# High and low activation parts side by side, and the last up projection with one wide high-weight matmul per block

## The chip, the cores and the metric

The kernel runs on one core of one Trainium2 chip. The number of interest is the device time of one launch in microseconds (us). TensorE (PE in the profile, its weight loads PEld) multiplies, VectorE (DVE), ScalarE (ACT) and GpSimd (POOL) do the elementwise work, SyncE (SP) issues the weight transfers.

## The reference

Three layers run on one sequence of 256 tokens and 1024 features, in float32: two layers of a first block (retention and differential attention, each with a memory attention beside it) and one layer of a second block (a state-space mixer beside forgetting attention). Each layer ends with a gated MLP. The change is in the last one:

```python
def conv_gated_mlp(x, w_up, conv_w, conv_b, w_down):
    h = x @ w_up.astype(x.dtype)
    h = causal_depthwise_conv(h, conv_w, conv_b)
    gate, val = jnp.split(h, 2, axis=-1)
    return (jax.nn.silu(gate) * val) @ w_down.astype(x.dtype)
```

Its input is `rms_norm_2(x, norm_ffn_w)`, `w_up` is 1024 x 5632, the convolution has 3 taps along the tokens and a bias, `w_down` is 2816 x 1024.

## The kernel before

Activations lie feature-major: 128 features on the partitions, T = 256 tokens along the row. Every weight is split into a rounded high part and the rest (low), every activation too, and a product is high x high + high x low + low x high, all in the format fp32r (the trace prints it as f32 or fp32r). For each block of 128 input features TensorE therefore has two forms in `products`:

- **separate** (L728, L729, L730): high weight on the high activation, high weight on the low activation, low weight on the high activation: three matmuls of 256 columns with three weight loads, all summed in one half of a PSUM bank;
- **joined** (L726, L730): the high weight goes over both activation parts at once, 512 columns, and leaves two sums in the two halves of the bank; then the low weight on the high activation, 256 columns. Two weight loads. Somebody has to add the two halves afterwards.

The joined form is used for the names in `HALVES`: the up projections of the first two layers and most of the down projections. All high parts of a buffer lie in its first half and all low parts in its second; `hi_and_lo` makes the view of 512 columns out of two runs of 256.

A projection goes through its weight tiles one by one (`project` on TensorE). `up2`, the last up projection, has 44 weight tiles of 8 blocks, gate and value tiles in turn, four tiles per turn of a loop, the first turn written out. While tile c is evacuated, the engines do this for it:

- SyncE loads the raw weight tile into a ring of 4. ScalarE rounds it to the high part (`split_hi`, L1163), VectorE subtracts (`split_lo`, L1653), both three tiles ahead of TensorE.
- VectorE evacuates the sum of tile c times the reciprocal root mean square (`rstd`) into one of two rows of `halo` (`halo_evac`, L1794).
- ScalarE does the last tap and the bias (`last_tap`, L1266), VectorE the other two taps of tile c-1 (`other_taps`, L1803, twice; the second waits for the first), and then `split_lo`.
- On value tiles ScalarE also takes the silu of the gate tile before (L1239) and rounds the product of the pair before (`ffn_split`, L1234); GpSimd multiplies silu and value (L1596) and subtracts the rounded product (`lo`, L1573), once per pair of tiles. `down2` reads what comes out.

Each engine works strictly in the order written; what it waits for are counters (semaphores). In the first two layers' up projections (`up0`, `up1`) ScalarE copies the second half of the PSUM bank to `low_half` (`copy_low`, L1246), VectorE adds (L1771, L1775), and GpSimd multiplies by the root (L1581).

Of the kernel before, what the change touches and what calls it, by code (L numbers as in the profile page):

```python
# [23 lines left out]
P = 128  # L24
T = 256
# [90 lines left out]
HALVES = ("up0", "up1", "down0", "down1", "down2")  # L116
# [218 lines left out]
def program(nc, x_in, mem_in, params_in, consts_in, w, out):  # L335
# [9 lines left out]
    with ExitStack() as ctx:  # L345
# [11 lines left out]
        act_hi, act_lo = act_parts[:, 0:FT * T], act_parts[:, FT * T:2 * FT * T]  # L357
        xw_hi, xw_lo = xw_parts[:, 0:KT * T], xw_parts[:, KT * T:2 * KT * T]
# [11 lines left out]
        small_r = act_hi[:, 20 * T:22 * T]  # L370
# [73 lines left out]
        x_first, low_copied, gate_summed, silu_scaled = sem("x_first"), sem("low_copied"), sem("gate_summed"), sem("silu_scaled")  # L444
# [57 lines left out]
        def tok(buf, c0, width, tt):  # L502
# [4 lines left out]
        NORMS = [("mem", "kv", act_hi, act_lo), ("attn0", "in0", xw_hi, xw_lo), ("ffn0", "up0", xw_hi, xw_lo),  # L507
                 ("attn1", "in1", xw_hi, xw_lo), ("ffn1", "up1", xw_hi, xw_lo), ("mix2", "in2", xw_hi, xw_lo),
                 ("ffn2", "up2", xw_hi, xw_lo)]
# [207 lines left out]
        def _(pe):  # L717
            mm = nc.tensor.matmul

            def products(ps, a, parts, t, start, stop, halves=False):  # L720


                w_hi, w_lo = ring_hi[:, a:a + P], ring_lo[:, a:a + P]
                x_parts = hi_and_lo(parts, t * T)
                if halves:
                    mm(ps[:, 0:2 * T], w_hi, x_parts, start=start, stop=False)  # L726
                else:
                    mm(ps[:, 0:T], w_hi, x_parts[:, 0, :], start=start, stop=False)  # L728
                    mm(ps[:, 0:T], w_hi, x_parts[:, 1, :], start=False, stop=False)  # L729
                return mm(ps[:, 0:T], w_lo, x_parts[:, 0, :], start=False, stop=stop)  # L730

            def project(ph, i, c, parts, ready, halfway=None):
# [12 lines left out]
                if ph.by_token(c):  # L745
                    second = c not in ph.wide
                    for k in range(4):
                        if halfway and k == 2:
                            halfway(c)
                        t = ph.inputs[4 * second + k]  # L750
                        a = slot * DM + k * T
                        w_hi, w_lo = ring_hi[:, a:a + T], ring_lo[:, a:a + T]
                        for tt in range(2):
                            o = bank[b][:, tt * T:(tt + 1) * T]
                            x_tok = hi_and_lo(parts, t * T + tt * P, P)
                            mm(o, x_tok[:, 0, :], w_hi, start=not second and k == 0 and tt == 0, stop=False)  # L756
                            mm(o, x_tok[:, 0, :], w_lo, start=False, stop=False)  # L757
                            last = mm(o, x_tok[:, 1, :], w_hi, start=False, stop=second and k == 3 and tt == 1)  # L758
                    last.then_inc(tile_done, 1)
                    return  # L760
# [381 lines left out]
        def _(act):  # L1142
# [23 lines left out]
            def stream_hi(q, m, src):  # L1166
                name, _, hi, _ = NORMS[q]
                A(tile(hi, m), tile(src, m), ACT.Copy, scale=pcol(name, m)).then_inc(xh_done, 1)
# [24 lines left out]
            def run(name, after=None, q=None, unrolled=False, end=None):  # L1193

                ph = PH[name]
                peeled = ph.turns if unrolled else 1
                for i in range(peeled):
                    for c in range(ph.body):
                        for j, d in split_steps(ph, i, c):
                            split_hi(ph, j, d)  # L1200
                        if c == 0 and i == 0 and q is not None:
                            inverse_root(q)
                        if after:
                            after(ph, i, c)
                if peeled < ph.turns:
                    with act.Fori(peeled, ph.turns) as i:
                        for c in range(ph.body):
                            split_hi(ph, i, c)
# [23 lines left out]
            def ffn_split(p, h, f):  # L1232
                act.wait_ge(prod_done, p + 1)
                A(tile(act_hi, f), two(prod, h), ACT.Copy).then_inc(ffn_hi, 1)  # L1234
# [6 lines left out]
            def copy_low(layer, ph, i, c):  # L1241

                act.wait_ge(tile_done, ph.tile(i, c)[1] + 1)
                if not (type(i) is int and c < 2):
                    act.wait_ge(out_ready, ph.out(i, c) - 1)
                A(two(low_half, c % 2), bank[ph.bank(i, c)][:, T:2 * T], ACT.Copy).then_inc(low_copied, 1)  # L1246

            def swiglu(layer):
                def after(ph, i, c):
                    h = c // 2  # L1250
                    p = FT * layer + 2 * i + h
                    copy_low(layer, ph, i, c)
# [7 lines left out]
            def last_tap(n, taps, j, n_conv, b):  # L1260

                act.wait_ge(out_ready, n + 1)
# [114 lines left out]
            def values(layer, kind, h):  # L1377
# [8 lines left out]
                A(tile(act_hi, t - 12), bank[6][:, 0:T], ACT.Copy).then_inc(vals_hi, 1)  # L1386

            def mix(layer, k):

                t = mixed_tile(act, layer, k)  # L1390
                A(tile(act_hi, k), tile(u, t), ACT.Copy).then_inc(mix_hi, 1)

            def mix_high(layer, k):

                t = mixed_tile(act, layer, k)
                A(tile(act_hi, k, 2 * T), tile(u, t, 2 * T), ACT.Copy).then_inc(pair_hi, 1)
# [56 lines left out]
            def fox_values(layer, p):  # L1453
                act.wait_ge(fx_o, p + 1)
                A(tile(act_hi, 8 + p), bank[6][:, 0:T], ACT.Copy).then_inc(fx_hi, 1)
# [92 lines left out]
            run("up2", conv_swiglu, 6, end=lambda: ffn_split(3 * FT - 1, 1, FT - 1))  # L1548
# [4 lines left out]
        def _(pool):  # L1553
# [17 lines left out]
            def lo(p, h, f):  # L1571
                pool.wait_ge(ffn_hi, p + 1)
                G.tensor_tensor(tile(act_lo, f), two(prod, h), tile(act_hi, f).bitcast(f32), SUB).then_inc(ffn_lo, 1)  # L1573
# [15 lines left out]
            def conv_ffn():  # L1589
                def product(i, h):  # L1590
# [6 lines left out]
                    lo(p, h, 2 * i + h)  # L1597
                for h in range(2):
                    product(0, h)
                with pool.Fori(1, FT // 2) as i:  # L1600
                    for h in range(2):
                        product(i, h)

            def mix(layer, k):
                pool.wait_ge(mix_hi, number["mix", (layer, k)] + 1)
                G.tensor_tensor(tile(act_lo, k), tile(u, mixed_tile(None, layer, k)),
                                tile(act_hi, k).bitcast(f32), SUB).then_inc(mix_lo, 1)
# [30 lines left out]
        def _(dve):  # L1638
# [151 lines left out]

            def halo_evac(ph, i, c, ps):
# [121 lines left out]
            def mix_low(layer, k):  # L1913
# [3 lines left out]
                V.tensor_tensor(tile(act_lo, k, 2 * T), tile(u, t, 2 * T), tile(act_hi, k, 2 * T).bitcast(f32),  # L1917
# [133 lines left out]
            def fox_values(layer, p):  # L2051
                dve.wait_ge(fx_hi, p + 1)
                V.tensor_tensor(tile(act_lo, 8 + p), bank[6][:, 0:T], tile(act_hi, 8 + p).bitcast(f32),
# [95 lines left out]
            run("up2", halo_evac, None, 6, before_split=conv_before, end=conv_end)  # L2149
# [105 lines left out]
```

## Time and profile before

| | |
|---|---|
| median of 3 runs | 1058.32 us (1050.75 to 1058.38) |
| profiled execution | 1054.23 us |
| its span in the trace | 1052.4 us |
| TensorE busy | 1033.7 us (98%) |
| VectorE busy | 792.3 us (75%) |
| ScalarE busy | 636.9 us (61%) |
| GpSimd busy | 233.8 us (22%) |
| `up2` on TensorE | 858.40 to 985.54 us |

The granted TensorE clock is 1.00 of full speed in every stretch asked for, and in the page's row of slices. Matmul durations in the trace contain the time in the pipe, so what one costs in a stream is read from start to start. A span on VectorE, ScalarE or GpSimd is likewise longer than the distance to the next start by 0.04 to 0.10 us.

### The profile page before, as it was taken

How to read it: one execution, taken by the hardware profiler on the slowest of the kernel's cores; microseconds unless marked ns; L12 is line 12 of the kernel's file. 1: busy time of each engine (PE TensorE's matmuls, PEld its weight loads, DVE VectorE, ACT ScalarE, POOL GpSimd, SP SyncE). 2: the span in 40 equal slices, each digit the busy share in tenths (PEclk: the TensorE clock that was granted, in tenths of full speed). 3: DMA queues.
4: the chain of work that ended last, by engine and by line, in shares of the span. 5: the costliest groups of instructions: out<-in, count | busy, mean ns of one | idle time of the engine just before them, and what ended most of it. 6: DMA issues, size and time to landing. Idle time of an engine off the chain costs nothing.

```text
span 1052.4 us, 22106 instructions
## 1 busy us (share of the span) xinstructions
PE 1033.7 (98%) x7484; PEld 945.9 (90%) x7484; DVE 792.3 (75%) x1315; ACT 636.9 (61%) x1188; POOL 233.8 (22%) x204
## 2 busy tenths in 40 slices
PE   7999999999999999999999998999999999999998
PEld 7999988888889888888888898999898999999888
DVE  6875897777665878987786668878867579888853
ACT  7654775665545676766665446665666666666532
POOL 3200044454110000244452110000101034444300
PEclk9999999999999999999999999999999999999999
DMA  8543476556665332666566654443343456555563
GB/s 296 181 138 94 132 221 196 182 180 187 188 187 180 126 106 72 200 200 193 185 184 196 187 174 158 148 156 121 114 128 120 128 166 190 179 179 179 169 211 101
DMA packets 52484, 174.37 MB, mean 166 GB/s; under 512 B 5952, under 2 KB 7232, under 8 KB 52288
## 3 DMA queue, kind: packets, MB, share of 16 engines
q1 hardware_dynamic: 52416, 173.46, 52.6%
q8 instruction: 44, 0.72, 0.3%
q14 instruction: 24, 0.20, 0.1%
HBM read 172.39 MB, written 1.05 MB: 165 GB/s over the span
## 4 chain that ended last, share of the span: by engine, by line
PE 73%; DVE 13%; issue 6%; ACT 4%; DVEq 1%; DMA 1%; POOL 0%; ACTq 0%; SPq 0%; POOLq 0%
PE scores L726 14%; PE bank L730 13%; PE bank L726 12%; PE bank L728 8%; PE scores L730 7%; PE bank L729 7%; DVE tmp L1803 5%; DVE ring_parts L1653 3%; PE bank L756 2%; PE bank L757 1%; PE bank L758 1%; DVE con L1794 1%; ACT ring_parts L1163 1%; PE scores L971 1%; DMA ring_raw<-w_up 1%
## 5 line engine op out<-in xcount | busy, mean ns | idle before, releaser
L1653 DVE TENSOR_TENSOR ring_parts<-ring_raw,ring_parts 128x1024 fp32r<-128x1024 f32 (+2 forms) x343 | 421.8, 1232 | 38.3 <-ACT ring_parts L1163 32.1
L1163 ACT ACTIVATE ring_parts<-ring_raw 128x1024 fp32r<-128x1024 f32 (+2 forms) x343 | 341.0, 998 | 62.7 <-PE scores L730 29.3
L730 PE MATMUL bank<-xw_parts,ring_parts 128*128 128x256 f32 x1048 | 295.3, 282 | 0.0
L728 PE MATMUL bank<-xw_parts,ring_parts 128*128 128x256 f32 x696 | 202.6, 291 | 1.1 <-DVE ring_parts L1653 0.6
L730 PEld LDWEIGHTS bank<-xw_parts,ring_parts 128*128 128x128 f32 x1048 | 199.6, 190 | 0.0
L729 PE MATMUL bank<-xw_parts,ring_parts 128*128 128x256 f32 x696 | 196.7, 283 | 0.0
L730 PE MATMUL scores<-xw_parts,ring_parts 128*128 128x256 f32 x528 | 148.5, 281 | 0.0
L728 PEld LDWEIGHTS bank<-xw_parts,ring_parts 128*128 128x128 f32 x696 | 133.0, 191 | 6.8 <-issue 5.1
L730 PE MATMUL bank<-act_parts,ring_parts 128*128 128x256 f32 x480 | 135.2, 282 | 0.0
L729 PEld LDWEIGHTS bank<-xw_parts,ring_parts 128*128 128x128 f32 x696 | 133.1, 191 | 0.1
L726 PE MATMUL scores<-xw_parts,ring_parts 128*128 128x512 f32 x352 | 125.0, 397 | 0.6 <-DVE xw_parts L1659 0.6
L726 PE MATMUL bank<-xw_parts,ring_parts 128*128 128x512 f32 x352 | 124.5, 395 | 0.4 <-DVE xw_parts L1659 0.4
L730 PEld LDWEIGHTS scores<-xw_parts,ring_parts 128*128 128x128 f32 x528 | 100.3, 190 | 0.1
L1573 POOL TENSOR_TENSOR act_parts<-tmp,act_parts 128x256 f32 (+1 forms) x66 | 61.6, 934 | 168.6 <-ACT act_parts L1234 168.6
L730 PE MATMUL scores<-act_parts,ring_parts 128*128 128x256 f32 x336 | 94.4, 281 | 0.0
L726 PE MATMUL scores<-act_parts,ring_parts 128*128 128x512 f32 x264 | 93.1, 396 | 0.7 <-DVE ring_parts L1653 0.7
L730 PEld LDWEIGHTS bank<-act_parts,ring_parts 128*128 128x128 f32 x480 | 91.4, 190 | 0.0
L728 PE MATMUL bank<-act_parts,ring_parts 128*128 128x256 f32 x282 | 81.5, 289 | 2.7 <-DVE ring_parts L2098 1.4
L726 PEld LDWEIGHTS scores<-xw_parts,ring_parts 128*128 128x128 f32 x352 | 66.0, 187 | 16.5 <-DVE xw_parts L1659 1.2
L726 PEld LDWEIGHTS bank<-xw_parts,ring_parts 128*128 128x128 f32 x352 | 66.0, 187 | 16.2 <-DVE xw_parts L1659 0.9
L729 PE MATMUL bank<-act_parts,ring_parts 128*128 128x256 f32 x282 | 79.7, 283 | 0.0
L1581 POOL TENSOR_TENSOR tmp<-tmp,rstd 128x256 f32<-128x256 f32 x44 | 74.2, 1688 | 9.3 <-ACT tmp L1239 9.2
(245 smaller groups left out, 1928.8 us busy)
## 6 DMA issues: line engine op xcount, KB each, us to landing
ring_raw<-w_up SPq DMA_DIRECT2D x132, 512.0 KB, 3.6
ring_raw<-w_in SPq DMA_DIRECT2D x85, 512.0 KB, 3.5
ring_raw<-w_down SPq DMA_DIRECT2D x48, 512.0 KB, 3.6
ring_raw<-w_down SPq DMA_DIRECT2D x24, 384.0 KB, 4.0
ring_raw<-w_oa SPq DMA_DIRECT2D x16, 256.0 KB, 2.6
ring_raw<-w_ob SPq DMA_DIRECT2D x16, 256.0 KB, 2.9
ring_raw<-w_oa SPq DMA_DIRECT2D x8, 512.0 KB, 3.5
ring_raw<-w_ob SPq DMA_DIRECT2D x8, 512.0 KB, 3.5
```

The costliest lines, as they stand in the source:

```text
L726: mm(ps[:, 0:2 * T], w_hi, x_parts, start=start, stop=False)
L728: mm(ps[:, 0:T], w_hi, x_parts[:, 0, :], start=start, stop=False)
L729: mm(ps[:, 0:T], w_hi, x_parts[:, 1, :], start=False, stop=False)
L730: return mm(ps[:, 0:T], w_lo, x_parts[:, 0, :], start=False, stop=stop)
L756: mm(o, x_tok[:, 0, :], w_hi, start=not second and k == 0 and tt == 0, stop=False)
L757: mm(o, x_tok[:, 0, :], w_lo, start=False, stop=False)
L758: last = mm(o, x_tok[:, 1, :], w_hi, start=False, stop=second and k == 3 and tt == 1)
L1163: A(ring_hi[:, slot * DM:slot * DM + width], ring_raw[:, slot * DM:slot * DM + width], ACT.Copy).then_inc(hi_done, 1)
L1573: G.tensor_tensor(tile(act_lo, f), two(prod, h), tile(act_hi, f).bitcast(f32), SUB).then_inc(ffn_lo, 1)
L1581: G.tensor_tensor(two(gate_s, h), two(gate_s, h), rstd[:, :], MUL).then_inc(silu_scaled, 1)
L1653: V.tensor_tensor(ring_lo[:, a:b], ring_raw[:, a:b], ring_hi[:, a:b].bitcast(f32), SUB).then_inc(lo_done, 1)
L1803: V.scalar_tensor_tensor(dst, halo[:, b * 264 + 3 - s:b * 264 + 259 - s], pcol(wname, j * taps + taps - 2 - s), acc, MUL, ADD).then_inc(do ...
```

## The change

1. The parts buffers are laid out anew: the high part of a tile (256 columns) is followed by its low part. The 512 columns of a joined matmul are now one run. `high`, `low`, `pair_of` and `pair_tiles` take the place of `hi_and_lo` and the two half buffers, in all stages. Which instructions run is not touched by this.
2. `up2` joins `HALVES`. TensorE uses the joined form. ScalarE copies the second half of the bank at the start of each tile's work (`first=copy_low`). VectorE adds the halves into `halo` (`halo_sum`) where it multiplied by the root. GpSimd multiplies the row by the root in place (`scaled`), and ScalarE's last tap waits for that.
3. GpSimd's order in `up2`: the product and the subtraction of a pair come one pair later, between the `scaled` of the next two tiles.

```diff
-HALVES = ("up0", "up1", "down0", "down1", "down2")
+HALVES = ("up0", "up1", "up2", "down0", "down1", "down2")
...
-        def hi_and_lo(parts, a, width=T):
-
-            return parts[:, :].rearrange("p (n c) -> p n c", n=2)[:, :, a:a + width]
+        def high(parts, k):
+
+            return parts[:, ds(k * (2 * T), T)]
+
+        def low(parts, k):
+            return parts[:, ds(k * (2 * T) + T, T)]
...
-                x_parts = hi_and_lo(parts, t * T)
                 if halves:
-                    mm(ps[:, 0:2 * T], w_hi, x_parts, start=start, stop=False)
+                    mm(ps[:, 0:2 * T], w_hi, tile(parts, 2 * t, 2 * T), start=start, stop=False)
...
                     with act.Fori(peeled, ph.turns) as i:
                         for c in range(ph.body):
+                            if first:
+                                first(ph, i, c)
                             split_hi(ph, i, c)
...
-                act.wait_ge(out_ready, n + 1)
+                if taps == 4:
+                    act.wait_ge(out_ready, n + 1)
+                else:
+                    act.wait_ge(halo_scaled, j + 1)
...
-            run("up2", conv_swiglu, 6, end=lambda: ffn_split(3 * FT - 1, 1, FT - 1))
+            run("up2", conv_swiglu, 6, end=lambda: ffn_split(3 * FT - 1, 1, FT - 1), first=copy_low)
...
             def conv_ffn():
+                def scaled(i, c):
+                    n = 4 * i + c
+                    pool.wait_ge(out_ready, PH["up2"].out0 + n + 1)
+                    row = halo[:, (c % 2) * 264 + 4:(c % 2) * 264 + 260]
+                    G.tensor_tensor(row, row, rstd[:, :], MUL).then_inc(halo_scaled, 1)
+
...
-                    lo(p, h, 2 * i + h)
+
+                def pair(i, h):
+
+                    before = not (type(i) is int and i == 0 and h == 0)
+                    scaled(i, 2 * h)
+                    if before:
+                        product(i if h else i - 1, 1 - h)
+                    scaled(i, 2 * h + 1)
+                    if before:
+                        lo(2 * FT + 2 * i + h - 1, 1 - h, 2 * i + h - 1)
...
+            def halo_sum(ph, i, c, ps):
+                b = c % 2
+                dve.wait_ge(low_copied, 4 * FT + 4 * i + c + 1)
+                V.tensor_tensor(halo[:, b * 264 + 4:b * 264 + 260], ps, two(low_half, b), ADD).then_inc(out_ready, 1)
...
-            run("up2", halo_evac, None, 6, before_split=conv_before, end=conv_end)
+            run("up2", halo_sum, None, 6, before_split=conv_before, end=conv_end)
```

ScalarE's order in the first turn of `up2`, tiles 1 to 3, before (L1163 `split_hi`, L1239 silu, L1234 `ffn_split`, L1266 last tap):

```order
L1163 ACTIVATE ring_parts<-ring_raw 128x1024 [waits tile_done,w_loaded2]
L1266 ACTIVATE tmp<-con,par 128x256 [waits conv_b,out_ready]
L1163 ACTIVATE ring_parts<-ring_raw 128x1024 [waits tile_done,w_loaded3]
L1239 ACTIVATE tmp<-tmp 128x256 [waits prod_done,conv_d]
L1234 ACTIVATE act_parts<-tmp 128x256 [waits prod_done]
L1266 ACTIVATE tmp<-con,par 128x256 [waits conv_b,out_ready]
```

And now (L1171 `split_hi`, L1253 silu, L1248 `ffn_split`, L1283 last tap, L1260 `copy_low`):

```order
L1260 ACTIVATE u<-scores 128x256 [waits out_ready,tile_done]
L1171 ACTIVATE ring_parts<-ring_raw 128x1024 [waits tile_done,w_loaded2]
L1283 ACTIVATE tmp<-con,par 128x256 [waits conv_b,halo_scaled]
L1260 ACTIVATE u<-bank 128x256 [waits out_ready,tile_done]
L1171 ACTIVATE ring_parts<-ring_raw 128x1024 [waits tile_done,w_loaded3]
L1253 ACTIVATE tmp<-tmp 128x256 [waits prod_done,conv_d]
L1248 ACTIVATE act_parts<-tmp 128x256 [waits prod_done]
L1283 ACTIVATE tmp<-con,par 128x256 [waits conv_b,halo_scaled]
```

A copy stands ahead of each `split_hi`, behind the last tap of the tile before, and the last tap waits for GpSimd instead of VectorE.

GpSimd's order in the first turn of `up2`, before (L1569 is the last work ahead of it, L1596 the product, L1573 `lo`):

```order
L1569 TENSOR_TENSOR scratch<-scratch 128x256 [waits ss_done,sq_done] x7
L1596 TENSOR_TENSOR tmp<-tmp 128x256 [waits conv_d,silu_done]
L1573 TENSOR_TENSOR act_parts<-tmp,act_parts 128x256 [waits ffn_hi]
L1596 TENSOR_TENSOR tmp<-tmp 128x256 [waits conv_d,silu_done]
L1573 TENSOR_TENSOR act_parts<-tmp,act_parts 128x256 [waits ffn_hi]
```

And now (L1611 `scaled`, L1619 the product, L1590 `lo`):

```order
L1586 TENSOR_TENSOR scratch<-scratch 128x256 [waits ss_done,sq_done] x7
L1611 TENSOR_TENSOR con<-con,rstd 128x256 [waits out_ready] x3
L1619 TENSOR_TENSOR tmp<-tmp 128x256 [waits conv_d,silu_done]
L1611 TENSOR_TENSOR con<-con,rstd 128x256 [waits out_ready]
L1590 TENSOR_TENSOR act_parts<-tmp,act_parts 128x256 [waits ffn_hi]
```

Two instructions per pair of tiles have become four, each with two inputs in SBUF.

## Rows read from the trace of the kernel before

**Rows 1.** The page: busy time and share, and the chain by engine

```profile
PE 1033.7 (98%) x7484; PEld 945.9 (90%) x7484; DVE 792.3 (75%) x1315; ACT 636.9 (61%) x1188; POOL 233.8 (22%) x204
PE 73%; DVE 13%; issue 6%; ACT 4%; DVEq 1%; DMA 1%; POOL 0%; ACTq 0%; SPq 0%; POOLq 0%
```

**Rows 2.** Windows in `up0` and `up2`: PE, PEld, DVE, ACT, POOL, clock, DMA

```profile
150.00:220.00 70.00, 70.00 (x398) 60.68 (x397) 55.73 (x76) 43.82 (x76) 34.05 (x26) 1.00 0.59 188
870.00:985.00 115.00, 115.00 (x961) 115.00 (x960) 102.96 (x159) 71.80 (x121) 53.94 (x40) 1.00 0.58 181
```

**Rows 3.** Timeline of PE: start, duration; `up2` separate, to `down2`'s first

```profile
913.54 0.28 PE L728 MATMUL bank<-xw_parts,ring_parts 128*128 128x256 f32 x1
...
919.30 0.28 PE L728 MATMUL scores<-xw_parts,ring_parts 128*128 128x256 f32 x1
...
985.54 0.40 PE L726 MATMUL bank<-act_parts,ring_parts 128*128 128x512 f32 x1
```

**Rows 4.** Timeline of PE in `up0`, joined

```profile
175.99 0.40 PE L726 MATMUL scores<-xw_parts,ring_parts 128*128 128x512 f32 x1
176.22 0.28 PE L730 MATMUL scores<-xw_parts,ring_parts 128*128 128x256 f32 x1
...
181.64 0.40 PE L726 MATMUL bank<-xw_parts,ring_parts 128*128 128x512 f32 x1
```

**Rows 5.** Timeline of PE: one run of 384 columns, then two of 128

```profile
686.04 0.33 PE L1081 MATMUL bank<-act_parts,pick_r 128*128 128x384 f32 x1
686.21 0.28 PE L1082 MATMUL bank<-ident_r,mask_r 128*128 128x256 f32 x1
686.33 0.28 PE L728 MATMUL bank<-xw_parts,ring_parts 128*128 128x256 f32 x1
```

**Rows 6.** Timeline of DVE in `up2`: start, duration; one tile, then the next

```profile
908.59 0.42 DVE L1794 TENSOR_TENSOR con<-bank,rstd 128x256 f32<-128x256 f32 x1
908.92 0.63 DVE L1803 SCALAR_TENSOR_TENSOR tmp<-con,par,tmp 128x256 f32<-128x256 f32 x1
909.70 0.48 DVE L1803 SCALAR_TENSOR_TENSOR tmp<-con,par,tmp 128x256 f32<-128x256 f32 x1 [0.15 <-DVE tmp L1803]
910.31 1.23 DVE L1653 TENSOR_TENSOR ring_parts<-ring_raw,ring_parts 128x1024 fp32r<-128x1024 f32 x1
911.45 0.42 DVE L1794 TENSOR_TENSOR con<-scores,rstd 128x256 f32<-128x256 f32 x1
```

**Rows 7.** Timeline of POOL: `up2` beside VectorE, and the stage's last

```profile
908.29 0.97 POOL L1573 TENSOR_TENSOR act_parts<-tmp,act_parts 128x256 f32 x1 [1.89 <-ACT act_parts L1234]
910.34 1.78 POOL L1596 TENSOR_TENSOR tmp<-tmp 128x256 f32<-128x256 f32 x1 [1.08 <-DVE tmp L1803]
...
992.81 0.73 POOL L1573 TENSOR_TENSOR act_parts<-tmp,act_parts 128x256 f32 x1 [0.72 <-ACT act_parts L1234]
```

**Rows 8.** Timeline of ACT: `copy_low` in `up0`; silu to `split_hi` in `up2`

```profile
176.27 0.39 ACT L1246 ACTIVATE u<-bank 128x256 f32<-128x256 f32 x1 [1.36 <-PE bank L730]
...
913.28 0.42 ACT L1239 ACTIVATE tmp<-tmp 128x256 f32<-128x256 f32 x1 [2.32 <-DVE tmp L1803]
913.91 0.59 ACT L1266 ACTIVATE tmp<-con,par 128x256 f32<-128x256 f32 x1
914.40 1.04 ACT L1163 ACTIVATE ring_parts<-ring_raw 128x1024 fp32r<-128x1024 f32 x1
```

**Rows 9.** Timeline of DVE in `up0`: a sum, and `split_lo` beside POOL

```profile
176.69 0.42 DVE L1771 TENSOR_TENSOR tmp<-bank,u 128x256 f32<-128x256 f32 x1 [0.94 <-ACT u L1246]
...
177.49 1.76 DVE L1653 TENSOR_TENSOR ring_parts<-ring_raw,ring_parts 128x1024 fp32r<-128x1024 f32 x1
```

**Rows 10.** Timeline of POOL in `up0`: the instruction beside it

```profile
177.25 0.92 POOL L1573 TENSOR_TENSOR act_parts<-tmp,act_parts 128x256 f32 x1 [3.12 <-ACT act_parts L1234]
```

**Rows 11.** Timeline of DVE: `up2`'s first and last evacuation

```profile
864.39 0.42 DVE L1794 TENSOR_TENSOR con<-bank,rstd 128x256 f32<-128x256 f32 x1
...
986.84 0.42 DVE L1794 TENSOR_TENSOR con<-bank,rstd 128x256 f32<-128x256 f32 x1
```

More of the change, by code:

```diff
@@ L503, in tok @@
             return buf[:, tt * DM + c0:tt * DM + c0 + width]
-        NORMS = [("mem", "kv", act_hi, act_lo), ("attn0", "in0", xw_hi, xw_lo), ("ffn0", "up0", xw_hi, xw_lo),
-                 ("attn1", "in1", xw_hi, xw_lo), ("ffn1", "up1", xw_hi, xw_lo), ("mix2", "in2", xw_hi, xw_lo),
-                 ("ffn2", "up2", xw_hi, xw_lo)]
+        NORMS = [("mem", "kv", act_parts), ("attn0", "in0", xw_parts), ("ffn0", "up0", xw_parts),
+                 ("attn1", "in1", xw_parts), ("ffn1", "up1", xw_parts), ("mix2", "in2", xw_parts),
+                 ("ffn2", "up2", xw_parts)]
         LAST_Q = {0: 1, 1: 3, 2: 5}
@@ L754, in project @@
                             o = bank[b][:, tt * T:(tt + 1) * T]
[L755 to L758, printed above, removed]
+                            x_hi, x_lo = (m(parts, t)[:, tt * P:(tt + 1) * P] for m in (high, low))
+                            mm(o, x_hi, w_hi, start=not second and k == 0 and tt == 0, stop=False)
+                            mm(o, x_hi, w_lo, start=False, stop=False)
+                            last = mm(o, x_lo, w_hi, start=False, stop=second and k == 3 and tt == 1)
                     last.then_inc(tile_done, 1)
@@ L1191, in inverse_root, with run @@
                 A(rstd[:, :], logs, ACT.Exp, scale=-0.5).then_inc(root_done, 1)
-            def run(name, after=None, q=None, unrolled=False, end=None):
+            def run(name, after=None, q=None, unrolled=False, end=None, first=None):
                 ph = PH[name]
@@ L1198, in run @@
                     for c in range(ph.body):
+                        if first and (i or c):
+                            first(ph, i, c)
                         for j, d in split_steps(ph, i, c):
@@ L1202, in run @@
                             inverse_root(q)
+                            if first:
+                                first(ph, i, c)
                         if after:
@@ L1207, in run @@
                         for c in range(ph.body):
+                            if first:
+                                first(ph, i, c)
                             split_hi(ph, i, c)
@@ L1233, in ffn_split @@
                 act.wait_ge(prod_done, p + 1)
-                A(tile(act_hi, f), two(prod, h), ACT.Copy).then_inc(ffn_hi, 1)
+                A(high(act_parts, f), two(prod, h), ACT.Copy).then_inc(ffn_hi, 1)
             def silu_gate(p, h, src):
@@ L1251, in after @@
                     p = FT * layer + 2 * i + h
-                    copy_low(layer, ph, i, c)
+                    copy_low(ph, i, c)
                     if c % 2 == 0:
@@ L1454, in fox_values @@
                 act.wait_ge(fx_o, p + 1)
-                A(tile(act_hi, 8 + p), bank[6][:, 0:T], ACT.Copy).then_inc(fx_hi, 1)
+                A(high(act_parts, 8 + p), bank[6][:, 0:T], ACT.Copy).then_inc(fx_hi, 1)
             def fox_weights(layer, p):
@@ L1572, in lo @@
                 pool.wait_ge(ffn_hi, p + 1)
-                G.tensor_tensor(tile(act_lo, f), two(prod, h), tile(act_hi, f).bitcast(f32), SUB).then_inc(ffn_lo, 1)
+                G.tensor_tensor(low(act_parts, f), two(prod, h), high(act_parts, f).bitcast(f32), SUB).then_inc(ffn_lo, 1)
             def ffn(layer):
```

49 lines of the change are left out of this document (27 added, 22 removed).

## The prediction, made before the changed kernel ran

> **What bounds the kernel now.** I read the page first. TensorE is busy 98% of the span and carries 73% of the chain of waits; VectorE carries 13% [rows 1]. That says "TensorE" for the whole, but the change puts its new work into `up2`, so the windows come next: in a stretch of `up2` TensorE is busy all 115 us, and VectorE 103 of 115, against 56 of 70 in `up0` [rows 2]. Then the timelines, engine by engine.
>
> TensorE in `up2` goes from one tile pair to the next in 919.30 - 913.54 = 5.76 us, 48 matmuls of 0.120 us each [rows 3]. In `up0` the joined form takes 181.64 - 175.99 = 5.65 us for 32 matmuls [rows 4], so a joined tile costs 2.82 us and a separate one 2.88. That is all that joining can give as measured: 0.055 x 44 = 2.4 us.
>
> VectorE does one tile of `up2` in 911.45 - 908.59 = 2.86 us, four instructions with one gap of 0.15 us [rows 6]. It is as slow as TensorE. Whatever lengthens its step sets the pace of the stage.
>
> Why a step is 2.86: the first of the two taps takes 0.63 us, the second 0.48 [rows 6]. While the first runs, GpSimd is finishing an instruction that began at 908.29 and ends at 909.26; the tap ends 0.29 us after that, at 909.55 [rows 6, 7]. The reverse is seen too: GpSimd's product starts at 910.34, 0.03 us after `split_lo`, and takes 1.78 us where an undisturbed GpSimd instruction takes 0.73; it ends 0.58 us after `split_lo` does (912.12 against 911.54) [rows 6, 7]. In `up0` a `split_lo` that starts 0.24 us after a GpSimd instruction takes 1.76 us in place of 1.23, and ends 1.08 us after it [rows 6, 9, 10]. So an instruction of GpSimd and one of VectorE with two inputs in SBUF go one after the other. VectorE's evacuation has one input in PSUM, takes 0.42 us beside GpSimd's product, and is free of this [rows 6, 7].
>
> **The change, part by part.**
>
> *TensorE in `up2`*: 44 tiles at 2.82 in place of 2.88, at best -2.4 us. It is worth nothing if VectorE's step is longer than 2.82, and it is already.
>
> *VectorE*: the multiplication by the root becomes a sum of the same shape with one input in PSUM, 0.42 us as in `up0` [rows 9]. No count changes.
>
> *GpSimd*: 44 instructions more, `scaled`, each 0.73 us alone. Two per pair of tiles have become four, and all of them take turns with the taps and `split_lo`.
>
> *ScalarE*: 44 copies of 0.39 us [rows 8]. ScalarE has time for 44 x 0.39 = 17 us (72 of 115 busy, [rows 2]), but the copy of tile c stands behind the last tap of tile c-1, and VectorE's sum of tile c waits for it.
>
> I lay out a pair of steps, t = 0 at the start of VectorE's sum.
>
> *Gate tile*: tap 1 starts at 0.33 and ends at 0.82 (0.48 when undisturbed). `scaled` waits from 0.58 (the sum's end plus 0.16, as the product starts 0.16 after the tap's end at 910.18). Between the two taps there is the gap of 0.15 us, so GpSimd goes in and ends at 0.82 + 0.58 = 1.40. Tap 2 ends 0.29 later, 1.69. `split_lo` starts 0.13 later (910.31 - 910.18), 1.82, and the next sum 1.14 after that (911.45 - 910.31): **2.96 us**.
>
> *Value tile*: `split_lo` of the step before ends at 0.09 by this tile's clock, so the product ends at 0.67 and tap 1 at 0.96; `scaled`, behind the product, ends at 1.54; tap 2 at 1.83. ScalarE starts the silu 0.12 later at 1.95, the last tap 0.63 after that (913.91 - 913.28) at 2.58, the next tile's copy 0.49 later (914.40 - 913.91) at 3.07; it ends at 3.46, and VectorE sums 0.03 later (176.69 against 176.66) [rows 8, 9]: **3.49 us**. VectorE alone would be free at 3.10; the other 0.39 is the chain through ScalarE.
>
> A pair is 6.45 us. From the first to the last evacuation of `up2` it is now 986.84 - 864.39 = 122.4 us [rows 11]; 43 steps become 21.5 x 6.45 = 138.7, **+16.3 us**. Does the end pass it on? `down2` starts on TensorE at 985.54 [rows 3], comes to its last two blocks after some 20 x 0.353 = 7.1 us and needs them by 993; the last of them is ready at 992.81 + 0.73 = 993.54 [rows 7]. There is no slack, so it passes on in full. The bounds: if GpSimd's instructions cost VectorE nothing beyond today's, the gate step is 2.86 and the value step 0.33 + 0.63 + 0.15 + 0.48 = 1.59, plus the same 1.66 through ScalarE, 3.25: a pair of 6.11, +9.0 us. If the product gets in ahead of `split_lo` (they start 0.03 us apart) it costs VectorE 0.53 more per pair, as in `up0`: +27 us. The register instructions that the new waits bring are in no row; the gap of 0.15 us in a loop shows their size, once or so per pair, up to +3 us. I take +16.3, since each of its terms is the duration of the same instruction beside the same neighbour.
>
> *The layout*: 1166 joined matmuls outside `up2` (2 x 352 in `up0` and `up1`, 3 x 154 in the down projections, by the code) read one run of 512 columns in place of two of 256. No row shows such a read. A joined pair takes 0.353 us, of which L730 is 0.120 or a little less, so the wide one is 0.23 [rows 4]. From below: two runs of 128 (L1082) take 0.12 [rows 5], the same as one run of 256, so a second run costs nothing there. From above: one run of 384 takes 0.17 [rows 5]; 128 columns more at the full clock of 2.4 GHz (granted 1.00, [rows 2]) are 0.053, together 0.224, 0.01 under what is measured. So 0 to 10 ns each, 0 to 11.7 us. I take 3 ns, nearer to the row that has two runs in it: **-3.5 us**. Those stages would turn it into time, since TensorE bounds them: VectorE has 14 of 70 us free in `up0`.
>
> The Trainium skill (TensorE: Matmul & The Clock Gate, "Wait — 56ns, not 53.3ns?") gives a warm 512-column matmul 215.7 ns from start to start, without a word on how the columns lie. By it a joined pair is worth some 18 ns more than its row shows, and if the two runs are the reason the sum would be 21 us lower. The 0.120 us of every 256-column matmul, with one run, stand against 109 by the same formula, so the trace does not bear that out.
>
> *Sum*: 1054.2 (profiled execution) + 16.3 - 3.5 = **1067 us**. That execution is 4.1 us under the median of the runs; against the median the same sum gives 1071.
>
> **The rivals.**
>
> 1. *One run is read at the row of 384's rate* (10 ns each): 1054.2 + 16.3 - 11.7 = 1059. For it: the wide matmul carries twice the overhead of the one of 384. Against: two runs of 128 cost nothing extra. 25%.
> 2. *GpSimd's new instructions fit beside VectorE*, and only ScalarE's chain is left: 1054.2 + 9.0 - 3.5 = 1060. For it: `scaled` is issued while VectorE sums from PSUM. Against: it can start only when that sum has ended, and then tap 1 is ahead of it. 14%.
> 3. *Faster*: the four GpSimd instructions fall into VectorE's free moments, the value step shrinks to the undisturbed chain 0.33 + 2 x 0.5 + 1.66 = 2.99, TensorE's 5.65 per pair paces the stage (121.5 us, -0.9), and the layout gives its whole 11.7: 1042. It decides if VectorE's pair comes under 5.65; four turns of 0.58 us in the 0.66 us of two sums speak against it. 10%.
> 4. By the page's figure with the slow `up2`: 0.018 x 1166 = 21 us off, 1054.2 + 16.3 - 21 = 1049.5. 4%.
> 5. *The product overtakes `split_lo`*: 1054.2 + 27 - 3.5 = 1078. 5%.
>
> My forecast keeps 42%, its own range is 1063 to 1074 (layout 0 to 6 ns, registers up to 3 us).
>
> **The numbers.** 1050 to 1077 leaves out rivals 3 to 5 (19%) and takes in the two bounds of the layout and of the stage. What a measurement of this kernel can tell from no change is about 1%, 10.6 us. The forecast is +12.8, over that in most of its range (36 of 42), and rival 5 too; rival 1 at +4.8 and rival 2 at +5.8 lie within, with 7 of 39 over it if the layout gives less and the registers cost. Slower by over 1%: 0.48; within 1%: 0.40; faster by over 1%: 0.12 (rival 3 and part of 4).
>
> **What would show it.** In `up2` of the changed kernel: VectorE's distance from sum to sum 2.96 and 3.49 in turn; `scaled` 0.8 to 0.95 us long and ending between the taps; TensorE waiting in its tiles, VectorE waiting on ScalarE's copy on every second tile; the stage 16 us longer. In `up0`: a pair of tiles in 5.60 us for 3 ns, 5.49 for 10 ns, 5.65 if the layout does nothing. I am wrong if the pair of `up2` comes under 6.1 us, or if `up0` gains over 0.1 us per pair.

## The result, and the profile after

| | before | after |
|---|---|---|
| median, runs side by side on one chip | 1054.53 us (4 runs, 1050.29 to 1058.38) | 1067.49 us (4 runs, 1066.66 to 1070.41) |
| ratio to before | | 1.0138 (95% interval 1.0106 to 1.0169) |
| profiled execution, span | 1054.23, 1052.4 us | 1067.06, 1065.3 us |
| VectorE's first to last evacuation of `up2` | 122.45 us | 137.98 us |

The changed kernel is 13 us (1.4%) slower; 1067.0 was forecast. The interval of the ratio lies wholly above 1%.

The page of the changed kernel: busy time, then the chain by engine.

```profile
PE 1040.2 (98%) x7132; PEld 925.3 (87%) x7132; DVE 801.9 (75%) x1315; ACT 651.9 (61%) x1232; POOL 273.2 (26%) x248
PE 74%; DVE 12%; ACT 5%; issue 4%; DMA 1%; DVEq 1%; ACTq 1%; POOL 0%; SPq 0%; POOLq 0%
```

Beside [rows 1] this tells almost nothing. TensorE has 352 matmuls fewer (44 tiles of 8 blocks) and is still busy 98%, and GpSimd is on 0% of the chain. The windows, of `up0` and `up2` as in [rows 2], tell more:

```profile
150.00:220.00 70.00, 70.00 (x406) 61.22 (x406) 56.96 (x77) 44.12 (x76) 34.17 (x26) 1.00 0.62 192
870.00:998.00 128.00, 122.20 (x639) 97.07 (x638) 111.68 (x160) 85.23 (x160) 89.16 (x80) 1.00 0.51 161
```

In `up2` TensorE had no idle time and now idles 5.8 of 128 us; GpSimd has gone from 54 busy of 115 to 89 of 128. VectorE does 160 instructions in 128 us, before 159 in 115. The granted clock is 1.00 in both.

One pair of tiles on VectorE (start, duration, in brackets the idle time before and who ended it), as [rows 6]. L1828 is the sum, L1842 the two taps, L1687 `split_lo`:

```profile
922.55 0.42 DVE L1828 TENSOR_TENSOR con<-bank,u 128x256 f32<-128x256 f32 x1
922.89 0.62 DVE L1842 SCALAR_TENSOR_TENSOR tmp<-con,par,tmp 128x256 f32<-128x256 f32 x1
923.67 0.72 DVE L1842 SCALAR_TENSOR_TENSOR tmp<-con,par,tmp 128x256 f32<-128x256 f32 x1 [0.15 <-DVE tmp L1842]
924.51 1.23 DVE L1687 TENSOR_TENSOR ring_parts<-ring_raw,ring_parts 128x1024 fp32r<-128x1024 f32 x1
925.94 0.42 DVE L1828 TENSOR_TENSOR con<-bank,u 128x256 f32<-128x256 f32 x1 [0.21 <-ACT u L1260]
926.28 0.48 DVE L1842 SCALAR_TENSOR_TENSOR tmp<-con,par,tmp 128x256 f32<-128x256 f32 x1
926.91 0.73 DVE L1842 SCALAR_TENSOR_TENSOR tmp<-con,par,tmp 128x256 f32<-128x256 f32 x1 [0.15 <-DVE tmp L1842]
927.77 1.22 DVE L1687 TENSOR_TENSOR ring_parts<-ring_raw,ring_parts 128x1024 fp32r<-128x1024 f32 x1
928.91 0.42 DVE L1828 TENSOR_TENSOR con<-scores,u 128x256 f32<-128x256 f32 x1
```

GpSimd beside it, as [rows 7]: L1611 `scaled`, L1590 `lo`, L1619 the product.

```profile
923.19 0.92 POOL L1611 TENSOR_TENSOR con<-con,rstd 128x256 f32<-128x256 f32 x1
925.36 0.97 POOL L1590 TENSOR_TENSOR act_parts<-tmp,act_parts 128x256 f32 x1 [1.25 <-ACT act_parts L1248]
926.45 0.91 POOL L1611 TENSOR_TENSOR con<-con,rstd 128x256 f32<-128x256 f32 x1
927.81 1.78 POOL L1619 TENSOR_TENSOR tmp<-tmp 128x256 f32<-128x256 f32 x1 [0.45 <-DVE tmp L1842]
```

And ScalarE in the value step, as [rows 8]: silu, `ffn_split`, last tap, the next tile's copy.

```profile
924.42 0.42 ACT L1253 ACTIVATE tmp<-tmp 128x256 f32<-128x256 f32 x1 [1.36 <-DVE tmp L1842]
924.75 0.40 ACT L1248 ACTIVATE act_parts<-tmp 128x256 f32 x1
925.05 0.59 ACT L1283 ACTIVATE tmp<-con,par 128x256 f32<-128x256 f32 x1
925.55 0.36 ACT L1260 ACTIVATE u<-bank 128x256 f32<-128x256 f32 x1
```

The reader is to see three things. The second tap takes 0.72 us in every step, where it took 0.48: `scaled` starts 0.30 us after the first tap does and ends at 924.11, and the second tap ends 0.28 us later. The steps are 925.94 - 922.55 = 3.39 us (value; 3.51 on every second one) and 928.91 - 925.94 = 2.97 us (gate). And in the value step VectorE is free 0.21 us before ScalarE's copy is: that copy stands behind silu, `ffn_split` and last tap, and the first of them, the silu, waits for the second tap.

The waits of the same stretch, 870 to 998 us (total, times, longest):

```profile
ACT tmp L1283 <- POOL con L1611: 15.4, 20, 0.8
...
DVE con L1828 <- ACT u L1260: 5.6, 20, 0.5
PE scores L734 <- DVE ring_parts L1687: 3.2, 10, 0.5
...
PE bank L734 <- DVE ring_parts L1687: 1.9, 10, 0.3
```

The largest entry, ScalarE's 15.4 us for `scaled`, looks like the culprit and is not: it falls in gate steps, where ScalarE has time. The 5.6 us on VectorE are 20 times 0.28, once per value step.

The end of the stage: VectorE's last evacuation (the first is at 861.55), GpSimd's last subtraction, TensorE's first block of `down2`, and its wait for the last activation block.

```profile
999.53 0.42 DVE L1828 TENSOR_TENSOR con<-bank,u 128x256 f32<-128x256 f32 x1
```

```profile
1005.49 0.73 POOL L1590 TENSOR_TENSOR act_parts<-tmp,act_parts 128x256 fp32r<-128x256 f32 x1 [0.53 <-ACT act_parts L1248]
```

```profile
996.28 0.49 PE L734 MATMUL bank<-act_parts,ring_parts 128*128 128x512 f32 x1
...
1006.27 0.51 PE L734 MATMUL bank<-act_parts,ring_parts 128*128 128x512 f32 x1 [1.48 <-POOL act_parts L1590]
```

The last subtraction on GpSimd ends 6.69 us after the last evacuation began, before 6.70 [rows 7, 11]. So whatever VectorE loses in `up2` arrives at the end.

Where the 12.9 us of span came from: the first evacuation of `up2` is 2.84 us earlier (861.55 against 864.39), the 43 steps to the last take 15.53 us longer, and the rest 0.2.

### The profile page after: what moved, and what is told of

Its sections match the earlier page's. It is cut to its first block, busy times and chain, and to the rows that moved or that the text cites. A ratio compares the mean times of both kernels' runs of the same rounds, so it can differ in the third digit from the quotient of the medians.

```text
span 1065.3 us, 21665 instructions
## 1 busy us (share of the span) xinstructions
PE 1040.2 (98%) x7132; PEld 925.3 (87%) x7132; DVE 801.9 (75%) x1315; ACT 651.9 (61%) x1232; POOL 273.2 (26%) x248
## 4 chain that ended last, share of the span: by engine, by line
PE 74%; DVE 12%; ACT 5%; issue 4%; DMA 1%; DVEq 1%; ACTq 1%; POOL 0%; SPq 0%; POOLq 0%
PE scores L734 14%; PE bank L738 13%; PE bank L734 12%; PE bank L736 8%; PE scores L738 7%; PE bank L737 7%; DVE tmp L1842 5%; DVE ring_parts L1687 3%; PE bank L764 2%; PE bank L765 1%; PE bank L766 1%; ACT ring_parts L1171 1%; DMA ring_raw<-w_up 1%; PE scores L979 1%; DVE con L1828 1%
## 5 line engine op out<-in xcount | busy, mean ns | idle before, releaser
L1687 DVE TENSOR_TENSOR ring_parts<-ring_raw,ring_parts 128x1024 fp32r<-128x1024 f32 (+2 forms) x343 | 422.0, 1233 | 38.6 <-ACT ring_parts L1171 32.9
L1171 ACT ACTIVATE ring_parts<-ring_raw 128x1024 fp32r<-128x1024 f32 (+2 forms) x343 | 341.2, 998 | 62.8 <-PE scores L738 28.6
L738 PE MATMUL bank<-xw_parts,ring_parts 128*128 128x256 f32 x1048 | 293.6, 280 | 0.0
L738 PEld LDWEIGHTS bank<-xw_parts,ring_parts 128*128 128x128 f32 x1048 | 198.6, 189 | 0.0
L734 PE MATMUL scores<-xw_parts,ring_parts 128*128 128x512 f32 x528 | 188.8, 400 | 4.2 <-DVE ring_parts L1687 3.2
L734 PE MATMUL bank<-xw_parts,ring_parts 128*128 128x512 f32 x528 | 188.1, 399 | 3.5 <-DVE ring_parts L1687 2.4
L736 PE MATMUL bank<-xw_parts,ring_parts 128*128 128x256 f32 x520 | 152.8, 294 | 1.1 <-DVE ring_parts L1687 0.6
L737 PE MATMUL bank<-xw_parts,ring_parts 128*128 128x256 f32 x520 | 146.9, 282 | 0.0
L734 PEld LDWEIGHTS scores<-xw_parts,ring_parts 128*128 128x128 f32 x528 | 99.0, 188 | 33.3 <-issue 9.7
L734 PEld LDWEIGHTS bank<-xw_parts,ring_parts 128*128 128x128 f32 x528 | 99.0, 188 | 32.7 <-issue 9.1
L736 PEld LDWEIGHTS bank<-xw_parts,ring_parts 128*128 128x128 f32 x520 | 99.2, 191 | 6.8 <-issue 5.1
L1590 POOL TENSOR_TENSOR act_parts<-tmp,act_parts 128x256 f32 (+1 forms) x66 | 61.1, 926 | 151.9 <-ACT act_parts L1248 151.9
L737 PEld LDWEIGHTS bank<-xw_parts,ring_parts 128*128 128x128 f32 x520 | 99.3, 191 | 0.1
L738 PEld LDWEIGHTS scores<-xw_parts,ring_parts 128*128 128x128 f32 x528 | 99.3, 188 | 0.1
L1842 DVE SCALAR_TENSOR_TENSOR tmp<-con,par,tmp 128x256 f32<-128x256 f32 x124 | 73.8, 595 | 7.1 <-DVE tmp L1842 6.1
```

The lines of the kernel that those rows point to most:

```text
L734: mm(ps[:, 0:2 * T], w_hi, tile(parts, 2 * t, 2 * T), start=start, stop=False)
L736: mm(ps[:, 0:T], w_hi, high(parts, t), start=start, stop=False)
L737: mm(ps[:, 0:T], w_hi, low(parts, t), start=False, stop=False)
L738: return mm(ps[:, 0:T], w_lo, high(parts, t), start=False, stop=stop)
L1171: A(ring_hi[:, slot * DM:slot * DM + width], ring_raw[:, slot * DM:slot * DM + width], ACT.Copy).then_inc(hi_done, 1)
L1590: G.tensor_tensor(low(act_parts, f), two(prod, h), high(act_parts, f).bitcast(f32), SUB).then_inc(ffn_lo, 1)
```

## The experiments

Three steps had to be told apart: the turns of GpSimd with VectorE, the chain through ScalarE's copy, and the layout.

**e1, the layout alone**; `up2` stays separate, with the copies, `scaled` and GpSimd's new order taken back too.

```diff
-HALVES = ("up0", "up1", "up2", "down0", "down1", "down2")
+HALVES = ("up0", "up1", "down0", "down1", "down2")
...
-            run("up2", halo_sum, None, 6, before_split=conv_before, end=conv_end)
+            run("up2", halo_evac, None, 6, before_split=conv_before, end=conv_end)
```

> The new layout of the parts in all stages, the last up projection as before. Theory A (the layout gives nothing; a joined pair of matmuls has two rates, 0.353 and 0.347 us, which a stage falls into by chance): within 0.3% of before, and the stages show either rate in both kernels. Theory B (one run of 512 columns is read faster): every joined stage at 0.347 us per pair, 1166 pairs x 0.006 = 7 us or 0.7% faster than a before whose stages are all at 0.353.

Measured: 1054.67 us (12 runs) against 1054.74 (23 runs), ratio 1.0005 (0.9985 to 1.0025); `up2` 122.46 us. The interval leaves room for a gain of 1.6 us and a loss of 2.6, so neither the 3.5 us of the forecast nor the 7 of theory B is there.

**e2, the join alone**, in the old layout, with the copies, `scaled` and GpSimd's new order.

```diff
-HALVES = ("up0", "up1", "down0", "down1", "down2")
+HALVES = ("up0", "up1", "up2", "down0", "down1", "down2")
...
-            run("up2", halo_evac, None, 6, before_split=conv_before, end=conv_end)
+            run("up2", halo_sum, None, 6, before_split=conv_before, end=conv_end)
```

> The old layout in all stages, the last up projection joined with ScalarE's copy, VectorE's sum and GpSimd's multiplication by the root. Theory A: as slow as the whole change, +13 us or 1.2% over before, VectorE's steps 2.96 and 3.4 to 3.5 us in turn. Theory B: 7 us slower still than the whole change, since it loses the layout's gain, +20 us.

Measured: 1070.95 us (4 runs), ratio 1.0139 (1.0116 to 1.0163); `up2` 137.94 us, steps 2.96, 3.51, 2.97, 3.38. All of the loss is in the join. Its median is 3.5 us above the changed kernel's, but the stage takes the same in both (137.94 and 137.98 us); what differs in the profiled executions is the rate of the joined matmuls in the stages before (the table further down).

**e3, without `scaled`**: the change with GpSimd's 44 multiplications left out, so the root is left out of this projection, and the last tap waits for the sum.

```diff
-                if taps == 4:
-                    act.wait_ge(out_ready, n + 1)
-                else:
-                    act.wait_ge(halo_scaled, j + 1)
+                act.wait_ge(out_ready, n + 1)
...
-                    scaled(i, 2 * h)
...
-                    scaled(i, 2 * h + 1)
```

> The change without GpSimd's 44 multiplications by the root (the root is left out of this projection), the last tap waits for VectorE's sum. Theory A (GpSimd and VectorE take turns, and the chain through ScalarE adds to it): gate step 2.75, value step 3.25 us, a pair 6.0 in place of 6.35, so 21.5 x 0.35 = 7.5 us under the whole change, 5 us over before. Rival (the chain through ScalarE alone sets the step, GpSimd is hidden): as slow as the whole change, within 2 us.

Measured: 1059.65 us (10 runs), ratio 1.0040 (1.0022 to 1.0058); `up2` 126.24 us. VectorE, a value step that ends on the copy, then a gate step:

```profile
920.19 0.62 DVE L1837 SCALAR_TENSOR_TENSOR tmp<-con,par,tmp 128x256 f32<-128x256 f32 x1
920.96 0.48 DVE L1837 SCALAR_TENSOR_TENSOR tmp<-con,par,tmp 128x256 f32<-128x256 f32 x1 [0.15 <-DVE tmp L1837]
...
922.99 0.42 DVE L1823 TENSOR_TENSOR con<-bank,u 128x256 f32<-128x256 f32 x1 [0.20 <-ACT u L1260]
923.34 0.48 DVE L1837 SCALAR_TENSOR_TENSOR tmp<-con,par,tmp 128x256 f32<-128x256 f32 x1
...
925.72 0.42 DVE L1823 TENSOR_TENSOR con<-scores,u 128x256 f32<-128x256 f32 x1
```

The second tap is back at 0.48, and the steps are 0.22 to 0.25 us shorter than in the change (2.72, 3.29, 2.72, 3.14 in turn). The wait of 0.20 for the copy is still there. So the copies and the chain through ScalarE alone come to 126.24 - 122.45 = 3.8 us, net of the gate steps, which are 0.15 us shorter than before's 2.87, since GpSimd's `lo` slows no tap in them:

```profile
922.41 0.97 POOL L1587 TENSOR_TENSOR act_parts<-tmp,act_parts 128x256 f32 x1 [1.89 <-ACT act_parts L1248]
```

**e4, the last tap ahead of the silu**, to cut the chain from the second tap to the copy.

```diff
                 h = c // 2
+                last_tap(ph.out(i, c), 3, j, 12 + j, c % 2)
                 if c % 2 == 1:
...
-                last_tap(ph.out(i, c), 3, j, 12 + j, c % 2)
```

> The change with ScalarE's last tap ahead of silu and rounding, so that 0.49 us leave the chain from VectorE's second tap to the next tile's copy. Theory A: on value tiles the last tap waits for GpSimd until 1.67, silu starts at 2.16, the copy ends at 3.2: value step 3.2 in place of 3.45 on average, 21.5 x 0.25 = 5 us under the whole change. Rival (GpSimd and VectorE taking turns is all of it, the chain is hidden): within 1 us of the whole change.

Measured: 1071.52 us (4 runs), ratio 1.0161 (1.0134 to 1.0188); `up2` 140.82 us, 2.8 longer than in the change, where 5 us less were expected. ScalarE:

```profile
925.97 0.60 ACT L1283 ACTIVATE tmp<-con,par 128x256 f32<-128x256 f32 x1 [1.35 <-POOL con L1611]
926.48 0.40 ACT L1253 ACTIVATE tmp<-tmp 128x256 f32<-128x256 f32 x1
926.79 0.40 ACT L1248 ACTIVATE act_parts<-tmp 128x256 f32 x1
927.09 0.36 ACT L1260 ACTIVATE u<-bank 128x256 f32<-128x256 f32 x1
```

The last tap is released by `scaled` (924.74 to 925.66 on GpSimd) no sooner than 925.97, 0.03 us after the second tap's end, as the silu was in the change. The same four instructions follow one another up to the copy, in another order, and the sum starts 1.55 us after the second tap in both kernels. The value step stays at 3.38 and 3.47. But `ffn_split` comes 0.5 us later, `lo` behind it moves into the gate step (927.40 on GpSimd), and that step rose from 2.96 to 3.09 and 3.14. The expectation had `scaled` release the last tap 1.67 us after the sum's start and the copy end at 3.2; the tap came at 1.86 (the sum starts at 924.11) and the copy ended at 3.34.

**e5, the copy ahead of the last tap** on value steps, so the copy no longer waits for the last tap. (On ScalarE it still follows the silu and `ffn_split`.)

```diff
+                    if c == 1:
+                        copy_low(ph, i, 2)
+                    else:
+                        copy_ahead(ph, i)
                 last_tap(ph.out(i, c), 3, j, 12 + j, c % 2)
```

> The whole change, but on value tiles ScalarE copies the next tile's second half ahead of its last tap, so that the tap leaves the chain from VectorE's second tap to the next sum. Theory A (in the value step it is ScalarE's chain that VectorE waits for, in both steps the turns with GpSimd): gate step stays at 2.96, value step falls from 3.45 to VectorE's own 3.1 us, 21.5 x 0.35 = 7.5 us under the whole change, 6 us over before. Rival (GpSimd takes over as the releaser, as with the last tap first): within 2 us of the whole change.

Measured: 1066.18 us (4 runs) against 1054.34 (24 runs), ratio 1.0110 (1.0076 to 1.0144); `up2` 133.97 us. VectorE's sums:

```profile
924.02 0.42 DVE L1850 TENSOR_TENSOR con<-bank,u 128x256 f32<-128x256 f32 x1
...
927.11 0.42 DVE L1850 TENSOR_TENSOR con<-bank,u 128x256 f32<-128x256 f32 x1
```

The value step is down to 3.10 as expected, with no wait for ScalarE. The gate step rose to 3.10 and 3.14: `lo` comes later against the next sum, and pushes the first tap. Half of the expected gain went there; 4.0 us are left of it.

**e6, two blocks grouped** in the kernel before: wide, wide, low, low instead of wide, low, wide, low, in all joined stages. It came out of the traces' two rates (below).

```diff
+                if ph.halves(i, c):
+                    for k0 in range(0, ph.blocks[part], 2):
+                        for k in (k0, k0 + 1):
...
+                            mm(bank[b][:, 0:2 * T], ring_hi[:, a:a + P], hi_and_lo(parts, t * T), start=kk == 0, stop=False)
+                        for k in (k0, k0 + 1):
...
+                            last = mm(bank[b][:, 0:T], ring_lo[:, a:a + P], hi_and_lo(parts, t * T)[:, 0, :], start=False, stop=end)
```

> Before, with the joined matmuls taken two blocks at a time: two wide ones, then the two with the low weights. Theory A (the two rates of a joined pair, 0.353 and 0.347, come of how the two forms alternate): one rate in all stages, and the runs no longer fall into clusters 3.5 us apart; if it is the faster rate, 3.5 us under the median of before. Rival (the rates have nothing to do with the alternation): clusters at 1051, 1054.6 and 1058 us as before.

Measured: 1052.31 us (12 runs, 1051.33 to 1052.86), ratio 0.9988 (0.9973 to 1.0003): no difference in the median that can be told, but a spread of 1.5 us where before has 7.6.

**e7, TensorE's part of the join alone**: the kernel before with `up2` in `HALVES` and nothing else, so the second half of the bank is left out of the sum in `up2`.

```diff
-HALVES = ("up0", "up1", "down0", "down1", "down2")
+HALVES = ("up0", "up1", "up2", "down0", "down1", "down2")
```

> Before, with joined matmuls in the last up projection and nothing else: the second half of the bank (high weight on low activation) is left out of the sum there. Theory A (VectorE paces this stage at 2.87 us per tile): within 1 us of before, first to last evacuation 122.4 us. Rival (TensorE paces it): 2.4 to 5 us faster.

Measured: 1055.29 us (10 runs), ratio 1.0006 (0.9986 to 1.0025); `up2` 122.45 us. 352 matmuls fewer gain nothing, since VectorE's step of 2.87 paces the stage.

**e8, GpSimd's new instructions alone**: the kernel before with 44 multiplications of the same shape on GpSimd in the changed order, on scratch rows that no other engine waits for.

```diff
+                def scaled(i, c):
...
+                    G.tensor_tensor(sqsum if c % 2 else two(sq, 1), two(sq, 0), rstd[:, :], MUL).then_inc(halo_scaled, 1)
```

> Before, with 44 GpSimd multiplications of two unused rows in the last up projection, one after each of VectorE's evacuations, in the order that the change gives GpSimd; nobody waits for them. Theory A (the turns cost VectorE 0.24 us per instruction, whoever waits for it): VectorE's steps 3.1 in place of 2.87 to 2.99 us, 9.5 us or 0.9% slower. Rival (only what waits for GpSimd's result costs): as before.

Measured: 1061.84 us (5 runs), ratio 1.0068 (1.0044 to 1.0093); `up2` 131.67 us, +9.2. VectorE, then GpSimd:

```profile
921.76 0.42 DVE L1812 TENSOR_TENSOR con<-bank,rstd 128x256 f32<-128x256 f32 x1
922.10 0.62 DVE L1821 SCALAR_TENSOR_TENSOR tmp<-con,par,tmp 128x256 f32<-128x256 f32 x1
922.87 0.73 DVE L1821 SCALAR_TENSOR_TENSOR tmp<-con,par,tmp 128x256 f32<-128x256 f32 x1 [0.15 <-DVE tmp L1821]
...
924.86 0.42 DVE L1812 TENSOR_TENSOR con<-bank,rstd 128x256 f32<-128x256 f32 x1
```

```profile
922.40 0.92 POOL L1595 TENSOR_TENSOR scratch<-scratch,rstd 128x256 f32<-128x256 f32 x1
```

No tap waits for this instruction, and the second one still takes 0.73 us in place of 0.48. That is the turn itself, without any wait of the program. The median is 7.5 us above before's, the stage of the profiled execution 9.2; 9.5 was expected. The new order of GpSimd is in e8 too, but not the cause: e3 has that order without the 44 instructions, and its second tap takes 0.48.

The parts of the stage, each from its own kernel:

| kernel | first to last evacuation of `up2` | against before |
|---|---|---|
| before, e1, e7 | 122.45, 122.46, 122.45 us | 0 |
| e3: copies and chain, no `scaled` | 126.24 | +3.8 |
| e8: `scaled` alone | 131.67 | +9.2 |
| e5: all, the chain shortened | 133.97 | +11.5 |
| after, e2 | 137.98, 137.94 | +15.5 |
| e4 | 140.82 | +18.4 |

The two alone make 13.0; the other 2.5 us come only when both are there. Counted from e3 the sum is plainer: with `scaled` its steps of 2.72, 3.14 and 3.29 us become 2.97, 3.39 and 3.51, each longer by what the second tap takes more: `split_lo` stands behind that tap in gate steps, silu and copy in value steps.

## Why the forecast held, and where its steps did not

*The join on TensorE is worth nothing*: right, e7 alone shows it.

*VectorE and GpSimd take turns*: right, in place and size. Counted from the sum's start, `scaled` was to end at 1.40 us in the gate step and 1.54 in the value step, the second tap at 1.69 and 1.83; measured 1.42 and 1.56, 1.70 and 1.84. It was to take 0.8 to 0.95 us and takes 0.91 to 0.92. The Trainium skill (SBUF — State Buffer, "Who interferes with whom") says that a VectorE instruction with two SBUF inputs contends with a GpSimd instruction that reads SBUF, while one with at most one SBUF input, outside the modes that use both ports, does not. The trace agrees on both: 0.48 becomes 0.73 for the tap, and the sum, with one input in PSUM, stays at 0.41 to 0.43 us in all kernels, with the product beside it too (928.91 in the changed kernel).

*Gate step 2.96*: 2.96 to 2.97. *Value step 3.49*: 3.39 and 3.51 in turn. Through ScalarE, from the second tap's end to the next sum, 1.66 was forecast and 1.55 is measured at 924.39 to 925.94 (the silu starts 0.03 us after the tap, not 0.12). The other value step, once per turn of the loop, has the longer form: 3.51, with the silu 0.12 us after the tap. The forecast had read its 0.12 from such a step. *The stage*: +16.3 forecast, +15.5 measured: a pair is 6.42 on average, not 6.45, which makes most of the difference. The product stayed behind `split_lo` (927.81 against 927.77), so rival 5 did not come about. The term of up to 3 us for register instructions rested on a gap that does not show them: the 0.15 us between the two taps are there in every step, in both kernels. Before, one step in four has some 0.27 in their place; after, none has, so that term came to nothing on VectorE.

*The bound of the stage was mis-sized*: with GpSimd free of charge a pair was put at 6.11 us, +9.0 (rival 2). e3 measures 2.72 + 3.14 and 2.72 + 3.29, +3.8. The main error is the gate step: 2.86 was taken from before, but it contains a tap slowed by GpSimd's `lo` (0.63 in place of 0.48), and in e3 `lo` (922.41 to 923.38) falls under VectorE's wait and its sum, and slows no tap. That is 3.0 of the 5.2 us between 9.0 and 3.8; the value step (3.21 on average, not 3.25) is 0.8, and the other 1.4 lie in the first four steps, 10.4 us where two later pairs take 11.9. That rival's total of 1060 is near e3's 1059.65 only because the -3.5 stood beside it.

*The end passes it on*: right; TensorE waits 1.48 us for the last block where it waited 0.46.

*The layout, -3.5*: **this step was wrong, and its size came out right by chance.** In the profiled execution `up0` runs at 5.55 us per two tiles instead of 5.65 [rows 4], which lies where the forecast had put the sign of a saving of 3 to 10 ns, and `up0` with `down0` takes 177.46 us instead of 180.28 (from the first joined matmul to the first behind the last), which is the whole 2.8 us by which `up2` starts earlier. Yet e1 measures nothing. The reason shows in three kernels on TensorE, each time in a tile's first wide matmul and that of the tile after next, 16 blocks later. The changed kernel in `up0`:

```profile
181.13 0.39 PE L734 MATMUL bank<-xw_parts,ring_parts 128*128 128x512 f32 x1
...
186.68 0.39 PE L734 MATMUL scores<-xw_parts,ring_parts 128*128 128x512 f32 x1
```

e3, which has the new layout too, in `up0`:

```profile
182.06 0.40 PE L734 MATMUL bank<-xw_parts,ring_parts 128*128 128x512 f32 x1
...
187.71 0.40 PE L734 MATMUL scores<-xw_parts,ring_parts 128*128 128x512 f32 x1
```

And the kernel before, in the old layout, in `up1`:

```profile
500.49 0.39 PE L726 MATMUL bank<-xw_parts,ring_parts 128*128 128x512 f32 x1
...
506.04 0.39 PE L726 MATMUL scores<-xw_parts,ring_parts 128*128 128x512 f32 x1
```

5.55, 5.65 and 5.55 us. Joined matmuls run at one of two rates, 0.3467 or 0.3534 us per block, whatever the layout. Each stage pair (`up0` with `down0`, `up1` with `down1`) falls into one and keeps it. In `down2`, after TensorE's wait for the last activation block, e2 and e3 ran at the faster one, before, after, e1 and e7 at the slower. There the rate can change in midstage, at that wait: in e2 it is 0.3533 us per block ahead of it and 0.3466 behind it, in e7 0.346 and 0.3533.

The forecast had read its rate from `up0` of before alone; before's `up1` has the faster rate in the old layout.

| profiled execution | layout | `up0`, `down0` | `up1`, `down1` | span |
|---|---|---|---|---|
| before | old | 353.4 ns | 346.7 ns | 1052.4 us |
| e7 | old | 346.7 | 353.3 | 1052.7 |
| e1 | new | 346.7 | 346.8 | 1049.2 |
| after | new | 346.7 | 346.7 | 1065.3 |
| e2 | old | 353.3 | 353.3 | 1070.9 |
| e3 | new | 353.3 | 346.7 | 1057.6 |

e4 (new layout) had both pairs at the faster rate, e5 (new) and e8 (old) the slower in the first and the faster in the second. 506 joined blocks in a stage pair (352 + 154) times 6.7 ns are 3.4 us. Before's 24 runs beside e5 to e8 lie in three bunches, 1050.4 to 1051.5, 1053.9 to 1055.1 and 1057.2 to 1058.1, 3.3 us apart, which fits none, one or two pairs at the slower rate. The profiled executions of after and e1 share layout and rates in both pairs: 1067.06 - 1050.98 = 16.1 us, though from two series of runs. It is one execution of each, and the nearest there is to the join's price like for like; the sum's +16.3 without its second term stands beside it. The medians differ by less, 13.0 us, because three of the four runs of after lie where both pairs would be at the faster rate, and before's median lies in the middle bunch.

Of the chances, the 42% stood for what happened in `up2`. The Trainium skill (TensorE: Matmul & The Clock Gate, "Wait — 56ns, not 53.3ns?") gives 215.7 ns for a warm 512-column matmul. The trace does not reach it in either layout: 0.23 us from start to start at a granted clock of 1.00, so the saving worked out from that figure did not exist here.

No version tried is faster than the kernel before by more than the noise. The best is e6, which gives the kernel before one time instead of three, at a median that can't be told from it.

## What to carry to other kernels

Before work is moved from one elementwise engine to an idle one, look whether the moved instructions take turns with those of the engine that paces the stage, as two-input instructions in SBUF do on GpSimd and VectorE here: 44 GpSimd instructions for which no tap waited cost the stage 9.2 us. A saving on the busiest engine is worth nothing where a second engine's step is as long, and a copy placed behind another chain on its engine brings that chain onto the path. When a rate is read from one stage, read it in every stage that runs the same instructions, and in more than one execution, before a difference of 2% in it is put down to a change.

## What the runs showed of the hardware that was not expected

- A stream of 512- and 256-column matmuls in turn, each with its own weight load, has two lasting rates, 0.3534 and 0.3467 us per pair of them, at a granted clock of 1.00 in both. In the one profiled execution with two of each in a row (e6) there is one rate: the wide pairs start 0.70 us apart, 0.697 on average in all stages, 0.348 per block, and 12 runs lie within 1.5 us. What puts a stage into one rate or the other is open; seen to change it within a stage is only a wait of TensorE (`down2` in e2 and e7).

```profile
200.44 0.63 PE L769 MATMUL scores<-xw_parts,ring_parts 128*128 128x512 f32 x2
200.91 0.39 PE L774 MATMUL scores<-xw_parts,ring_parts 128*128 128x256 f32 x2
201.14 0.63 PE L769 MATMUL scores<-xw_parts,ring_parts 128*128 128x512 f32 x2
```

- Two runs of 256 columns and one run of 512 as the moving input take the same time: ratio 1.0005 (e1), and both rates occur with either layout.
- A GpSimd instruction of 256 columns with two SBUF inputs costs VectorE 0.24 us in a tap of the same size, and itself grows from 0.73 to 0.92 us beside one. Started just after a `split_lo` of 1.22 us (927.81 against 927.77) it takes 1.78.
